# One stage for input normalisation and projections: the first two column chunks projected while later tokens are still being normed

## The reference, cut to what matters

```
h = modulate(rmsnorm(x, norm1_g), sh1, sc1)     # x: 2048 tokens x 1024
z = h @ w_in                                    # 1024 x 2048: 16 chunks of 128 columns
u_a, q, k, v, u_c = split(z)                    # q, k: 4 chunks each
q, k = rope(rmsnorm(q)), rope(rmsnorm(k))       # per head of 64
...                                             # pooling, attention, state space, gates, experts
```

## Time and profile before

| | us |
|---|---|
| median of 3 runs | 3267.26 |
| lowest, highest | 3266.67, 3274.03 |
| the profiled execution | 3264.71 |
| its span, first to last instruction | 3262.9 |

### The profile page before, as it was taken

One profiled execution on the slowest core, in us unless ns is written; L12 is line 12 of the kernel. 1 busy time (PEld: TensorE's weight loads), 2 busy tenths in 40 slices (PEclk: granted clock), 3 DMA queues, 4 the chain that ended last, 5 costly groups with the idle time before them and its releaser, 6 DMA issues. The chain is left out here.

```text
span 3262.9 us, 41708 instructions
## 1 busy us (share of the span) xinstructions
PE 2854.5 (87%) x13494; PEld 2215.7 (68%) x13495; DVE 1980.3 (61%) x3048; ACT 1472.7 (45%) x2363; POOL 383.4 (12%) x297
## 2 busy tenths in 40 slices
PE   2699898999999997799996897995899999999994
PEld 2576676676777766577774675884677777777772
DVE  5546986454545464533362665225788888888883
ACT  3313554554545452322232333122466666666662
POOL 3101211000000001110010000110122222222211
PEclk9799999999999998898897998997899999999997
DMA  5273434222222215411115997443797997876864
GB/s 215 60 239 118 154 104 124 80 88 81 77 89 65 85 54 199 126 49 39 39 55 193 317 284 271 162 168 129 271 315 252 356 356 257 272 229 206 278 197 135
DMA packets 289052, 553.56 MB, mean 170 GB/s; under 512 B 30745, under 2 KB 97561, under 8 KB 284834
## 3 DMA queue, kind: packets, MB, share of 16 engines
q1 hardware_dynamic: 266866, 500.43, 44.5%
q0 software_dynamic: 14112, 51.39, 6.6%
q10 hardware_dynamic: 7952, 0.16, 0.1%
HBM read 417.16 MB, written 143.15 MB: 172 GB/s over the span
## 5 line engine op out<-in xcount | busy, mean ns | idle before, releaser
L2484 DVE TENSOR_TENSOR moe_w_lo<-moe_W,moe_w_hi 128x1024 fp32r<-128x1024 f32 x392 | 470.8, 1221 | 83.3 <-ACT moe_w_hi L2420 81.2
L2420 ACT CAST moe_w_hi<-moe_W 128x1024 fp32r (+1 forms) x392 | 410.3, 1052 | 147.0 <-PE moe_h1b L2351 75.2
L1658 PE MATMUL project_bank<-h_lo,w_hi 128*128 128x512 f32 x512 | 204.7, 400 | 0.0
L682 DVE TENSOR_SCALAR_CACHE_REDUCE att_S<-att_bank 128x512 f32<-128x512 f32 x192 | 125.0, 689 | 121.5 <-PE att_bank L470 121.5
L503 PE MATMUL att_bank<-h_hi,w_hi 128*128 128x512 f32 x384 | 171.6, 447 | 12.3 <-PEq L137 9.0
L2376 PE MATMUL moe_yb<-moe_W,moe_hT 128*128 x384 | 172.6, 592 | 0.0
L2349 PE MATMUL moe_h1b<-moe_w_hi,moe_xT_hi 128*128 128x512 f32 x384 | 156.9, 409 | 3.8 <-DVE moe_xT_lo L2495 3.8
L588 ACT ACTIVATE att_S<-att_S,att_nm 128x128 f32<-128x128 f32 (+15 forms) x128 | 154.1, 1206 | 0.0
L504 PE MATMUL att_bank<-h_lo,w_hi 128*128 128x512 f32 x384 | 153.5, 400 | 0.0
L505 PE MATMUL att_bank<-h_hi,w_lo 128*128 128x512 f32 x384 | 152.9, 398 | 0.0
L2350 PE MATMUL moe_h1b<-moe_w_lo,moe_xT_hi 128*128 128x512 f32 x384 | 152.6, 397 | 0.0
(11 more groups left out here) (461 smaller groups left out, 6958.6 us busy)
## 6 DMA issues: line engine op xcount, KB each, us to landing
moe_W<-in_moe_w SPq DMA_DIRECT2D x96, 2048.0 KB, 10.9
w_raw<-in_gate_w SPq DMA_DIRECT2D x48, 512.0 KB, 3.7
out_sg<-gateT SPq DMA_DIRECT2D x32, 768.0 KB, 8.1
gateT<-att_gates SPq DMA_DIRECT2D x48, 256.0 KB, 2.4
gateT<-gate_out SPq DMA_DIRECT2D x48, 256.0 KB, 2.3
front_w<-in_ada_w SPq DMA_DIRECT2D x8, 1024.0 KB, 7.8
front_x<-in_x SPq DMA_DIRECT2D x16, 512.0 KB, 6.4
w_raw<-in_w_in SPq DMA_DIRECT2D x16, 512.0 KB, 4.4
```

Source lines behind the costliest of these rows:

```text
L1658: pe.matmul(bank[n % 4][:], w_hi[b][:, k, :], low[:, k, at], start=False, stop=False)
L2420: nc.scalar.copy(w_hi[:, slot(p, first), :], raw(at, p)).then_inc(q["w13_high"], 1)
L2484: nc.vector.tensor_tensor(w_lo[:, own, :], raw(at, p), w_hi[:, own, :].bitcast(F32), ALU.subtract).then_inc(q["w1_low" if p < 4 else "w3_l ...
```

## The change

stage_front is gone; its work is done inside stage_project, which then starts the program.

- SP queues more ahead: of the eight 1 MB pieces seven have buffers (laid over tiles of h that are written later), so four pieces, four x tiles in turn with them, the constants, three more pieces and the first chunk's weights are issued without a wait. The second chunk's weights follow once the first are split.
- DVE scales the first x tiles between its adds, and splits the weights of chunks 0 and 1 there too.
- The first eight units are (chunk 0, chunk 1) for each token group, and six of them run while the next group is being normed: from the second group on, PE makes one turn of transposes for the new group and then a quarter of a unit of the group before. Transposes have four PSUM banks now, not seven.
- Seven z chunks come ahead of the q and k chunks, not six; the 32 q and k units stand together as units 28 to 59, and one z chunk ends the stage. `pieces_by` starts at unit 14 and runs at 2.47 pieces a unit, not from unit 7 at 2.1; `ROW_AT` is 18, 21, 24, 27, not 12, 16, 20, 23.

The core of the diff:

```diff
-    XR, AR, W = 8, 3, 2 * D
...
-                stage_front(nc, g, h_hi, [h_lo, h_lo1])
...
-    NZ = 6
+    NZ, NF = 7, 8
...
-    chunks = z[:NZ] + qk[:4] + z[NZ:NZ + 1] + qk[4:] + z[NZ + 1:]
+    chunks = z[:NZ] + qk + z[NZ:]
...
-    units = [(c, tb) for c in range(NC) for tb in range(TB)]
+    units = [(c, tb) for tb in range(TB) for c in range(2)] + [(c, tb) for c in range(2, NC) for tb in range(TB)]
...
-    ROW_AT = (12, 16, 20, 23)
+    ROW_AT = (18, 21, 24, 27)
+    XR, AR, W = 8, 7, 2 * D
...
-        return max(0, min(4 * KD, int((n - 6) * 2.1)))
+        return max(0, min(4 * KD, int((n - 13) * 2.47)))
...
+                for k in range(4):
+                    load_early(k)
+                    load_x(k)
+                sp.dma_start(g["consts"][:], g["const_pack"]).then_inc(f["consts"], 16)
+                for k in range(4, AR):
+                    load_early(k)
                 load_w(0)
...
+                    if n >= 4:
+                        pe.wait_ge(f["h_high"], n - 3)
+                        pe.wait_ge(f["raised"], n - 3)
...
+                        if n < NF:
+                            pe.wait_ge(f["h_split"], KD * (tb + 1))
...
+                for n in range(KD):
+                    turn(n)
+                pe.wait_ge(f["col_ready"], 1)
+                for n in range(KD, NT8):
+                    turn(n)
+                    tb, k = n // KD - 1, n % KD
+                    products(2 * tb + k // 4, k % 4 * 2, k % 4 * 2 + 2)
+                for n in range(2 * TB - 2, NU + 2):
...
+                for k in range(KD):
+                    add(k)
+                    if 2 <= k < 6:
+                        scale(k - 2)
+                    if k == 6:
+                        split(0)
+                split(1)
```

More of the change, by code:

```diff
@@ L1529, in stage_project @@
         q = {n: s.sem(n) for n in names}
+        front_names = ("c_ready consts exped col_summed col_ready squared rooted reduced scaled_pool scaled_dve turned h_high raised h_split added").split()
+        f = {n: s.sem(f"x_{n}") for n in front_names}
+        early_ready = [s.sem(f"early_ready{i}") for i in range(AR)]
+        x_ready = [s.sem(f"x_ready{i}") for i in range(XR)]
         z_stored = [s.sem("z_stored0"), s.sem("z_stored1")]
@@ L1596, in _ @@
                     if n < NU and is_z[n]:
[L1597 to L1599 removed]
+                        store_z(n)
                 for b in range(2):
@@ new lines, in products @@
+                def products(n, k0, k1):
+                    c, tb = units[n]
+                    if k0 == 0:
+                        if tb == 0:
+                            pe.wait_ge(q["w_split"], c + 1)
+                        if n < NF:
+                            pe.wait_ge(f["h_split"], KD * (tb + 1))
+                        free_bank(n - 4)
+                    b, high, low = c % 2, h_hi[tb // 2], h_lo[tb // 2]
+                    for k in range(k0, k1):
+                        pe.matmul(bank[n % 4][:], w_hi[b][:, k, :], high[:, k, at512(tb)], start=k == 0, stop=False)
+                        pe.matmul(bank[n % 4][:], w_hi[b][:, k, :], low[:, k, at512(tb)], start=False, stop=False)
+                        mm = pe.matmul(bank[n % 4][:], w_lo[b][:, k, :], high[:, k, at512(tb)], start=False, stop=k == KD - 1)
+                    if k1 == KD:
+                        mm.then_inc(q["summed"], 1)
@@ new lines, in _ @@
+                pe.wait_ge(f["consts"], 48)
+                pe.wait_ge(f["added"], KD)
+                for k in range(2 * KD):
+                    mm = pe.matmul(bank[0][:, k:k + 1], sums[:, k * P:(k + 1) * P], const(g, "ones")[:, 0:1], start=True, stop=True)
+                mm.then_inc(f["col_summed"], 1)
+                for n in range(KD):
[5 more added lines that the diff above has]
+                    products(2 * tb + k // 4, k % 4 * 2, k % 4 * 2 + 2)
@@ L1649, in _ @@
                     if n < NU:
[L1650 to L1660 removed]
+                        products(n, 0, KD)
                     if 1 <= n <= NU and not is_z[n - 1]:
@@ L2715, in program @@
         shared_room, weight_room = ExitStack(), ExitStack()
+        with nc.sbuf_tensor("early0", [P, KD * D], F32) as early0:
+            pass
         shared = sb("shared", [P, 2, KD, 512], F32R, shared_room)
```

359 lines of the change are left out of this document (166 added, 193 removed).

## The result

The changed kernel takes 3276.70 us in the median (3270.59 to 3280.00), the kernel before 3267.38 on the same chip (3257.69 to 3274.03): a ratio of 1.0026, 95% interval 1.0018 to 1.0034. It is 9.3 us slower, where 5.3 us less were forecast; it lies 0.7 us above the upper end of the range given, 3276. So 9.3 has to be explained, not the 15.3 between the profiles.

A forecast was written before the change was run, and what follows sets the result against it. PE was taken to bound units 0 to 23, DVE the q and k units. +14.0 up to the first q unit and -19.3 in the q and k units give -5.3 us: 3262.0 us on the median's scale, range 3248 to 3276.

The forecast's parts named there:

- The first add: At the start, DVE's first add begins at 20.8 us instead of 16.86, since silu(c)'s small packets take turns with SP's bulk.
- The rival with the late add: At the start, ACT's third load is held until SP's queue is empty, at about 28 us: +4, 3271 us; chance 0.11.
- the first product later than 75: Sign at the first token group: PE's first product was put near 69 us; later than 75 makes the forecast wrong.
- The adds: DVE's opening adds: seven more at 2.35 us and the first at 1.29 give 17.7, plus gaps, inversions, scaling and a split.
- The Trainium skill's rule: DMA queues at the start: by whole-packet draining, silu(c) comes no later than before, making the sum 4 us smaller.
- The groups: Interleaved token groups, first product to unit 6: two at 20.8 us and a last at 18.2, together 59.8; unit 6 at 129.0.
- the rival of half clock throughout: In the groups, holes keep PE at half clock: 82 us instead of 59.8, +17, 3284 us; chance 0.05.
- The rows: The four rows among plain units: PE waits 23 us against 6.1, matmuls cost 14.0; first q unit at 289.6, +14.0.
- The rival in which the rows keep pace: At the four rows, only the present wait of 6.1 us stays: -26.7, 3240.6 us; chance 0.14.
- The q and k units: The 32 units standing together lose DVE's hole of 12.7 us and the q store's wait of 6.6 us: -19.3.
- The rival that keeps the wait behind the 8 MB: In the q and k units, the wait behind the 8 MB stays in another q unit: +1.3, 3268.6 us; chance 0.10.
- The end of the stage: Behind the last q unit, the stage ends as in the kernel before, with one z chunk under DVE's tail.

## Why the prediction was wrong

By its steps, in us at the place of each:

- **The first add: wrong, and the step that failed.** It was put at 20.8, from an ACT that goes on at 18.5, when 64 small packets for each engine, those of c, have had their turns beside SP's. It came at 27.51. c's packets were through sooner than that: up to 12 us, 1022 small packets passed beside 639 large ones, and c was there at 13.7. But ACT doesn't go on with them. It is held by issuing its third load, and that was free only at 25.30, when 1947 of the 4096 small packets had passed. The earlier trace rows could be read both ways, since before the release at 14.65 fell together with c's landing and with SP's queue running empty. The run with two loads moved shows that the loads behind c are the cause, 9.5 us.
- **The rival with the late add** had ACT held until SP's queue is empty, at 28. ACT was let go at 25.30, and SP's queue was still 97% busy from there to 28, so this reading is wrong too, though it had the direction. It was given 0.11. Its price, +4, charges the delay one for one, and that is what happened: ACT was let go 6.8 later than forecast, the first raise came 7.15 later. A third reading fits both kernels. In the six traces of the changed kernel and its variants that leave these loads on ACT, 1905 to 1925 small packets had passed half a us before the hold ended; in the kernel before and its new order it was 1929 and 1935 at 14.10, also half a us before the end. So the hold seems to end at a count of small packets and not with c or with the bulk. No run varied that count, and what ends the hold stays open.
- **A sign of being wrong that the prediction named,** the first product later than 75, is met (76.60).
- **The adds: right in length.** From the first add to the last one's end it took 22.1, where 21.5 were forecast. Two of them take 3.02 instead of 2.35 while POOL scales beside them; the 3.7 put down for gaps, inversions, scaling and split left room.
- **The Trainium skill's rule** (DMA: Bandwidth & Descriptors, Queues, rings and completion order) is that an engine drains some 9 to 17 descriptors before it changes rings. This case's trace disagrees, if a packet that it counts is a descriptor: in ten windows of 0.32 us each from 22.24 us on, the two queues pass equal numbers every time, 16 to 24. What the prediction drew from the rule, that c comes no later than before, came true (13.7, against 14.4 before), but not for this reason: c was quick because SP's queue left room from 5 to 8 us. It did not matter either, since ACT was held by another load.
- **The groups: right to 1.3.** From first product to unit 6 it took 60.99 (21.26, 20.91, 18.82), forecast 59.8. With the first product 7.4 late, unit 6 was 8.6 late. The half clock at each group's start and its return within the group are as forecast; the rival of half clock throughout falls.
- **The rows: waits right, their matmuls and the units a little under.** 22.9 of waits against 23, though the parts were 4.9, 7.1, 4.0 and 6.9, not 5, 7, 3 and 8. The third row ran at half clock too. From unit 6 to the first q unit it took 163.1, forecast 160.6: 2.5 more. The rival in which the rows keep pace is what one unit's shift of the pieces makes of it, 21 us, not what this kernel does.
- **The q and k units: right.** 229.6 against 249.2, 19.6 gained where 19.3 were forecast, and the order alone does it. The rival that keeps the wait behind the 8 MB falls; the late stores six units later show that the mechanism is real and depends on where they are put.
- **The end of the stage: left out.** I had it end as before. It ends 2.1 later, since the merged stage clears the front part's semaphores at its one end.

The sum: 7.4 (late first product), 1.2 (groups), 2.5 (rows and units), -0.3 (q and k units) and 2.1 (clears) are 12.9, the way from -5.3 to +7.55. That the change stayed under the 9.8 us of the prediction (9.3) is no merit of it, since its sign was the wrong one. The failed step alone is more than half; with the two loads moved, and nothing else, the kernel takes 3267.01 us, within the range given. But even that is no gain to speak of, which the prediction had right: unit 6 starts 20 us earlier than six units behind the old front would end, and one more z chunk (22.5) and the rows take it back before the q units begin. The rows, with their waits and the slow matmuls, make 39.5 of the way from unit 6 to the first q unit (163.1 less 22 units of 5.62), and made 16.5 before.

## What to carry to other kernels

Tiny loads of four-byte elements that stood here in a second queue beside bulk loads moved at the pace of the bulk, one small packet for each large, and the engine that issued them was held with them: put them first, on the queue that carries the bulk, and read from the trace which instruction the engine stands in, not only which load it needs. When work is moved earlier, the schedules that were tuned to its old place (here the rows' pieces) must move with it, or they take the gain back; here that was worth as much as the move itself. And count what a stage's end does in series for each resource that is moved into it.

## What was not expected of the hardware

- A load of 4 KB took 13.0 us on ACT's queue beside SP's bulk, 2.3 us as the first load on SP's queue; the third of three such loads 29.7 against 3.9 us. And ACT stood 23.44 us in issuing the third.
- Two of DVE's adds of 128x2048 took 3.02 us instead of 2.35 while POOL scaled x beside them; a third, which began 0.07 us before POOL's scaling, took 2.35, and that scaling 5.00 instead of the 2.84 of later ones.
- About thirty semaphore clears in a row cost 2.1 us on the path.
- Without interleaving, with turns of transposes at most 0.89 us apart ahead of them, products began at full clock (0.48 us for the first, then 0.23 apart). In the changed kernel, behind 2.02 us of idle time, one turn and 2.31 us more of it, they began at half (97.86, 0.80), though the granted clock was 1.00 up to 96 us.
